# Latent attention: in the wide units the turning of the unit's weights goes ahead of the scores of the unit two ahead

## The reference

```
def mla_attention(q, k, v):           # q, k: (1, 1024, 8, 96), v: (1, 1024, 8, 64)
    for blk in range(8):              # 128 queries at a time
        qs, qe = blk * 128, (blk + 1) * 128
        logits = einsum(q[:, qs:qe], k[:, :qe]) / sqrt(96)
        logits = where(k_chunk <= q_chunk, logits, -inf)     # chunks of 64
        probs = softmax(logits)
        out[blk] = einsum(probs, v[:, :qe])
```

## Time and profile before

| | |
|---|---|
| time, median of 3 runs | 2462.61 us (2462.29 to 2464.19) |
| time of the profiled execution | 2461.41 us |
| its span | 2459.6 us |
| PE busy | 2414.8 us, 98% |
| DVE busy | 1704.7 us, 69% |
| ACT busy | 1049.3 us, 43% |
| turns of the units of the latent attention | from about 339.6 to 483.0 us of the span |

### The profile page before, as it was taken

One profiled execution on the slowest core, in us unless ns is written; L12 is line 12 of the kernel. 1 busy time (PEld: TensorE's weight loads), 2 busy tenths in 40 slices (PEclk: granted clock), 3 DMA queues, 4 the chain that ended last, 5 costly groups with the idle time before them and its releaser, 6 DMA issues.

```text
span 2459.6 us, 29759 instructions
## 1 busy us (share of the span) xinstructions
PE 2414.8 (98%) x11494; PEld 1918.0 (78%) x11494; DVE 1704.7 (69%) x2072; ACT 1049.3 (43%) x1495; POOL 139.1 (6%) x227
## 2 busy tenths in 40 slices
PE   8999999999999999999999999999999999999997
PEld 6887755588888888888788777788878888888885
DVE  5238787846877778698873665455588877786888
ACT  5225676624433333333542333343356333334336
POOL 1002100000000010000001000000001000100001
PEclk9999999999999999999999999999999999999999
DMA  6110000142433381600134122233444433715103
GB/s 222 50 43 22 2 1 1 52 139 107 148 121 120 103 307 54 220 1 18 52 101 150 43 78 70 73 133 134 148 150 175 171 103 103 267 41 193 48 1 137
DMA packets 76245, 252.22 MB, mean 103 GB/s; under 512 B 6320, under 2 KB 6368, under 8 KB 76080
## 3 DMA queue, kind: packets, MB, share of 16 engines
q1 hardware_dynamic: 43792, 131.08, 16.6%
q0 software_dynamic: 32320, 119.32, 13.0%
HBM read 186.78 MB, written 62.91 MB: 102 GB/s over the span
## 4 chain that ended last, share of the span: by engine, by line
PE 75%; DVE 10%; issue 4%; ACT 2%; DVEq 0%; ACTq 0%
PE ps L2717 23%; PE ps L3124 20%; PE ps L3162 18%; PE ps L3292 6%; DVE opQ_lo L2132 1%; DVE opQ_lo L2129 1%; DVE spot L2174 1%; DVE ql_raw L2169 1%; PE ps L3219 1%; PE ps L3238 1%; DVE Pb L2002 1%; PE ps L2965 1%; PE ps L3228 1%; PE ps L2839 0%; PE ps L3061 0%
## 5 line engine op out<-in xcount | busy, mean ns | idle before, releaser
L3162 PE MATMUL ps<-opQ_hi 128*128 128x512 f32 x896 | 350.3, 391 | 2.9 <-DVE opQ_lo L2132 2.9
L3162 PE MATMUL ps<-opQ_lo,opQ_hi 128*128 128x512 f32 x896 | 348.8, 389 | 0.0
L3162 PE MATMUL ps<-opQ_hi,opQ_lo 128*128 128x512 f32 x896 | 348.6, 389 | 0.0
L2717 PE MATMUL ps<-opP_hi,w_hi 128*128 128x512 f32 x638 | 199.0, 393 | 2.4 <-DVE w_lo L1620 0.8
L3162 PEld LDWEIGHTS ps<-opQ_hi 128*128 128x128 f32 x896 | 168.2, 188 | 42.3 <-DVE opQ_lo L2132 7.2
L2717 PE MATMUL ps<-opP_lo,w_hi 128*128 128x512 f32 x638 | 196.6, 389 | 0.0
L2717 PE MATMUL ps<-opP_hi,w_lo 128*128 128x512 f32 x638 | 196.5, 389 | 0.0
L3162 PEld LDWEIGHTS ps<-opQ_hi,opQ_lo 128*128 128x128 f32 x896 | 168.2, 188 | 35.0
L3162 PEld LDWEIGHTS ps<-opQ_lo,opQ_hi 128*128 128x128 f32 x896 | 168.2, 188 | 34.8 <-issue 0.2
L1276 ACT ACTIVATE opQ_hi<-spot 128x1024 fp32r<-128x1024 f32 x80 | 84.9, 1061 | 235.7 <-PE ps L3162 196.6
L884 ACT ACTIVATE w_hi<-w_stage 128x1024 fp32r<-128x1024 f32 x104 | 109.3, 1051 | 174.4 <-PE ps L2717 151.8
(11 more groups left out here) (441 smaller groups left out, 4755.1 us busy)
## 6 DMA issues: line engine op xcount, KB each, us to landing
w_stage<-in_w_stream SPq DMA_DIRECT2D x104, 512.0 KB, 3.6
h_spill<-T POOLq DMA_DIRECT2D x56, 512.0 KB, 4.5
pair_raw<-in_w_stream SPq DMA_DIRECT2D x26, 1024.0 KB, 5.8
spot<-in_w_stream SPq DMA_DIRECT2D x24, 1024.0 KB, 6.9
spot<-h_spill POOLq DMA_DIRECT2D x24, 1024.0 KB, 9.4
qh_raw<-in_w_stream SPq DMA_DIRECT2D x8, 1024.0 KB, 11.6
ql_raw<-h_spill POOLq DMA_DIRECT2D x8, 1024.0 KB, 7.5
g_spill<-T POOLq DMA_DIRECT2D x16, 512.0 KB, 2.9
```

The costliest lines, as they stand in the source:

```text
L2717: mm = pe.matmul(ps[:, psum + half, :], weight, operand[:, k, half * HALF:(half + 1) * HALF], start=(begin and x == 0 and weight is wh and ...
L3162: mm = pe.matmul(ps[:, down_bank(sc, f) + m, :], weight, operand, start=(g == 0 and kt == 0 and weight is wh and operand is hi), stop=(g = ...
```

## The change

In the wide units PE's order in a turn becomes T(u), S(u+2) instead of S(u+2), T(u). In narrow units it stays. The streams of DVE, ACT, POOL and SP are not touched, no instruction is added or taken away, and a V that stands in a wide turn is now the first thing in it.

```
             for u in range(len(QBLOCKS)):
                 if u == 0:
                     pe.wait_ge(mha["ke"], WIN)
-                for x in new_units(u):
-                    scores_of(x)
+                if narrow(u):
+                    for x in new_units(u):
+                        scores_of(x)
                 if u % 4 == 2 and 6 <= u < 60:
                     values((u - 6) // 4)
                 if u == 60:
                     values(14)
                 turn_weights(u)
+                if not narrow(u):
+                    for x in new_units(u):
+                        scores_of(x)
                 if u == 61:
                     pe.wait_ge(w_lo_done, B_WOUT + 1)
                     pe.wait_ge(evac_done, B_WOUT)
```

## The result

The changed kernel takes 2528.2 us, against 2462.3 us before, each the median of 5 runs in turns: 65.9 us more, a ratio of 1.0267 (95% interval 1.0256 to 1.0278). I had said 2504, with 2494 to 2514 as the range. The direction was right, the size was not: the loss is 1.6 times the one forecast.

What follows compares the result with a forecast made beforehand. PE, busy for 98% of the span, was taken as the bound; the four wide stretches growing from 81.63 to 123.5 us add 41.9 us to 2462.6, giving 2504.5, said as 2504, range 2494 to 2514.

Steps and rivals of the forecast that it cites:

- The chain: Wide units: T(u+1) needs normalise N(u+1), which DVE does after maximum M(u+2), which waits for scores S(u+2).
- The lags: PE's stand in wide turns from the end of S(u+2) to T(u+1), while DVE works: 0.97 to 2.37 us.
- The hand-overs: Within a wide turn's wait: 0.08 us from S's end to M's memset, 0.05 us from N's end to T.
- The sum: Wide turns at T + S + lag: four stretches grow from 81.63 to 123.5 us, +41.9 us, giving 2504.5.
- its term: The last pair's wide stretch, six turns 56 to 61: 27.2 us.
- One bound: Lower bound on the wait in wide turns: 0.2 to 0.3 us less per turn, about 8 us over 30 turns.
- The clock: PE's clock in the wide turns was taken to stay at 1.00, the upper level of 2.4 GHz.
- my second rival: PE's clock falls from many short stands: 2569 us if in all wide turns, 2537 if in half; chance 0.08.
- The signs: What the changed profile would show: wide stretches of 32 us, last one 27, normalise waits near 2 us, clock 1.00.
- A smaller lag: Rival: DVE starts sooner or work covers waits in wide turns; 2490 or 2483 us; chance 0.04.
- a faster kernel: Rival: earlier turnings and copies remove PE's small waits in the wide stretches, at most 3.8 us, 2459; chance 0.03.
- no change: Rival: slack behind the attention takes the loss back, 2463 us; chance 0.02.

Runs made afterwards that it cites:

- e1: The changed kernel, but in wide units DVE does normalise of u+1 ahead of maximum of u+2; 2474.5 us, ratio 1.0051.
- e5: The change in turns 10 and 14 of each pair alone (not in 62), all others in the old order; 2468.8 us, ratio 1.0024.
- e7: The changed kernel plus one useless matmul into a free bank behind the scores in turns 8, 10, 11 and 12, not turn 60; 2505.5 us, ratio 1.0175.
- e4: The change in the even wide turns alone (8, 10, 12, 14 of each pair), the odd ones in the old order; 2491.1 us, ratio 1.0114.

## Why the prediction missed, step by step

**The chain** was right and shown: S(u+2) -> M(u+2) -> N(u+1) -> T(u+1), cut in e1 (-54 us), covered in e5, visible with its four pieces in the timeline. The lags measured 1.90, 2.10, 2.17 and 2.30 us against 1.89, 2.09, 2.16 and 2.30 in the sum. The hand-overs of 0.08 and 0.05 us could be taken over as read.

**The sum** at full clock was right: 32.18 us for a stretch in e7 against 32.1, 2505.5 us for the whole kernel against 2504.5. That the last number agrees to 1 us is in part luck, since the last pair of e7 was 2.1 us over its term. One bound was misread: M's reduction and N's multiplication alone are 0.96 + 0.55 us of the lag of 1.89, so the lag could have been 0.38 us shorter for each turn and not 0.2 to 0.3, about 11 us in all and not 8. Nothing came of it, since the lag came out as read.

**The clock** is the step that failed: "So the sum is made at the upper level." The sum had 123.5 us for the four stretches; they took 148.25 at clocks of 0.78 to 0.84. It was my second rival, at a chance of 0.08, and the range left it out. In pair 0 the clock was down for a part of the turns 9, 11, 12 and 13 and stayed up in 8, 10, 14 and 15; the rival's 2569 us for all turns was too much, its 2537 for half of them near (2528). That it was so near is in part luck: the rival left out the products with the values, and the one with 24 matmuls grew from 2.60 to 4.29 us in pair 1. The evidence that I gave it so little on was one row, 335 to 340 us at a clock of 1.00. The same stretch, with the same instructions in front of and in it, in the trace of the changed kernel:

```profile
335.00:340.00 5.00, 2.98 (x11) 2.69 (x12) 2.45 (x9) 4.34 (x9) 0.00 (x0) 0.68 0.00 0
```

0.68 this time. Of the ten traces of this document eight have 1.00 in this window and two less, the changed kernel's and that of e5 (0.71), though no run changes anything that stands ahead of it. So such a stretch mostly stays up and now and then falls, and one row at 1.00 said little about thirty turns in a row. Why it fell in these two and not in the others is open, and so is why some of the wide turns fell and others not.

The prediction also had the Trainium skill speak against the change ("TensorE: Matmul & The Clock Gate", section "HAM oscillation — how this bites in real kernels"). The section tells of a kernel in which TensorE waited about 3 to 5 us for a DMA in each turn of its loop, and whose clock fell every time. No stand in a wide turn is longer than 2.3 us here, so that case is not this one, and the page doesn't settle it. The traces show that shorter stands can bring the clock down too, in some turns and not in all.

**The signs.** Forecast: the wait for `normalise` near 2 us in each of some 30 cases; it was 38.0 us in 22 waits, 15 of them of 1.90 to 2.30 us, since the products with the values cover T(10) nearly and T(14) wholly, and the projection's matmuls a part of T(62). Forecast: the wait for ACT's copy stays at 1.8 us; it became 6.4, 1.6 in each turn 8. The sum had this right, T(8) started when it did before and S(10) came behind it, but the sign did not: the waiting in the list grew because what had covered it moved away. Forecast: PE's busy time stays near 20 us in a stretch; it was 24.6 to 30.3, by the clock. "If the T row itself is longer, the clock is" wrong: that is what the row of 371.24 shows, 1.11 us for 0.66.

**The other rivals.** A smaller lag is excluded by the lags in the timeline, a faster kernel and no change by the time.

## What to carry to other kernels

Before two things on one engine are swapped, look up in the *other* engine's order what stands in front of the result that the first one needs, and count for every consumer the work between it and the last producer that it really hangs on. e4 shows that the count must be made for each consumer, the one in front of the moved work too. And when a change makes TensorE stand in every turn, the stand is not the whole price: its clock may fall, and the work itself grows longer; put that case into the range, whatever one short stretch of the old trace shows, and test it with a filler, which costs nothing as long as it lies inside the wait (in turn 8 of e7 it did, in turn 59 it didn't and cost 1 us).

## What the runs showed of the hardware

The clock fell with stands of no more than 2.3 us each: in the changed kernel PE was busy for 2.03 of the 3.93 us of turn 8, stood 1.90 us, and in turn 9 the clock was 0.68. One filler (a row of 1.02 us) in four turns of a pair was enough to hold it at 1.00 from T(8) to T(16) in the pairs 0 to 2; the second filler gave nothing more (2506.7 and 2505.5 us). A kernel became 22.7 us faster by doing useless work. The same instructions, at 335 to 340 us, ran at a granted clock of 1.00 in eight traces and at 0.68 and 0.71 in two.
